# Attention whose probabilities and outputs stay unscaled, with one table of sums that scales the outputs in the gate stage

## The reference, cut to what matters

```
p = jnp.exp(s - m)                                   # s: scores of one head, m: their row maximum
p = p / jnp.sum(p, axis=-1, keepdims=True)           # (guarded against zero)
o_a = einsum('bhqk,bkhd->bqhd', p, v)                # first kind: MLA, 8 heads

o = jnp.stack([o_c, o_s, o_w], axis=-2)              # first kind: NSA, 8 heads, three branches
o = jnp.einsum('bshnd,bshn->bshd', o, sigmoid(gate)) # each branch of each head has its own gate
x = x + (g_a * o_a + g_b * o_b + g_c * o_c) @ w_out  # merge; g_*: sigmoid of a wide product of h
```

## Time and profile before

| what | value |
|---|---|
| median of 3 runs | 3661.39 us (3660.16 to 3663.33) |
| the profiled execution, its span | 3659.4 us |
| what lies around the span, by the median | 2.0 us |
| PE busy | 3522.1 us, 96% |
| DVE busy | 2062.9 us, 56% |
| POOL busy | 1681.8 us, 46% |
| ACT busy | 1399.7 us, 38% |
| mean granted TensorE clock | 0.981 |

### The profile page before, as it was taken

How to read it: one execution, slowest core, us unless ns; L and a number is a source line. 1 busy time by engine, 2 the same in 40 slices (tenths; PEclk the granted TensorE clock), 3 DMA queues, 4 the chain that set the end, 5 groups by cost and what they waited for, 6 DMA issues and landing times. The chain is left out here.

```text
span 3659.4 us, 46833 instructions
## 1 busy us (share of the span) xinstructions
PE 3522.1 (96%) x16596; PEld 2873.6 (79%) x16596; DVE 2062.9 (56%) x3132; ACT 1399.7 (38%) x2450; POOL 1681.8 (46%) x949
## 2 busy tenths in 40 slices
PE   7999999999999999999999999989999999999998
PEld 6876878788878778777888778778877777778877
DVE  5777745212267777461123676558863666648953
ACT  3243652323233446433232436333333446333332
POOL 3347544344434375443444564425443655435543
PEclk9999999999999999999999999989999999999999
DMA  4310023222332110232243220533343220532322
GB/s 162 104 53 29 30 81 115 81 97 92 98 117 93 49 33 24 91 114 89 92 149 126 77 76 24 184 111 120 120 138 122 76 81 28 177 124 104 126 92 92
DMA packets 96756, 346.75 MB, mean 95 GB/s; under 512 B 12624, under 2 KB 13264, under 8 KB 95952
## 3 DMA queue, kind: packets, MB, share of 16 engines
q1 hardware_dynamic: 96592, 344.61, 27.8%
HBM read 338.14 MB, written 6.29 MB: 94 GB/s over the span
## 5 line engine op out<-in xcount | busy, mean ns | idle before, releaser
L226 POOL TENSOR_TENSOR weights_lo<-arena,weights_hi 128x1024 fp32r<-128x1024 f32 x467 | 1175.3, 2517 | 1529.9 <-ACT weights_hi L200 1528.9
L200 ACT ACTIVATE weights_hi<-arena 128x1024 fp32r<-128x1024 f32 x491 | 517.3, 1054 | 627.8 <-PE ps L634 389.8
L294 PE MATMUL ps<-moving_hi,weights_hi 128*128 128x512 f32 x2256 | 568.6, 394 | 11.7 <-ACT weights_hi L200 6.7
L294 PE MATMUL ps<-moving_lo,weights_hi 128*128 128x512 f32 x2256 | 558.5, 390 | 0.0
L294 PE MATMUL ps<-moving_hi,weights_lo 128*128 128x512 f32 x2256 | 558.0, 389 | 0.0
L294 PEld LDWEIGHTS ps<-moving_hi,weights_hi 128*128 128x128 f32 x2256 | 424.9, 189 | 103.5 <-ACT weights_hi L200 7.1
L294 PEld LDWEIGHTS ps<-moving_lo,weights_hi 128*128 128x128 f32 x2256 | 423.8, 188 | 87.6
L294 PEld LDWEIGHTS ps<-moving_hi,weights_lo 128*128 128x128 f32 x2256 | 423.2, 188 | 87.3
L1083 POOL TENSOR_SCALAR arena<-arena 128x128 f32<-128x128 f32 (+2 forms) x240 | 225.0, 950 | 211.0 <-DVE arena L988 131.8
L247 DVE TENSOR_TENSOR moving_lo<-arena,moving_hi 128x512 fp32r<-128x512 f32 x196 | 177.2, 955 | 233.5 <-ACT moving_hi L242 233.5
L2182 DVE SCALAR_TENSOR_TENSOR arena<-ps,arena 128x512 f32 x64 | 44.0, 691 | 306.7 <-PE ps L294 292.5
(11 more groups left out here) (366 smaller groups left out, 5587.2 us busy)
## 6 DMA issues: line engine op xcount, KB each, us to landing
arena<-wstream SPq DMA_DIRECT2D x532, 512.0 KB, 3.4
arena<-modw SPq DMA_DIRECT2D x64, 512.0 KB, 3.8
arena<-modw_first SPq DMA_DIRECT2D x32, 512.0 KB, 4.1
layer_input<-arena SPq DMA_DIRECT2D x2, 2048.0 KB, 6.9
arena<-layer_input SPq DMA_DIRECT2D x2, 2048.0 KB, 8.1
arena<-xT SPq DMA_DIRECT2D x4, 512.0 KB, 5.4
outT<-arena SPq DMA_DIRECT2D x8, 256.0 KB, 2.1
arena<-con SPq DMA_DIRECT2D x1, 1411.5 KB, 9.4
```

Of the source, the lines that this page charges most:

```text
L200: m.nc.scalar.activation(m.w_hi[:, j % 2, :], slab(m, base + at), ACT.Copy).then_inc(hi_ready, 1)
L226: m.nc.gpsimd.tensor_tensor(m.w_lo[:, j % 2, :], slab(m, base + (j if at is None else at)), m.w_hi[:, j % 2, :].bitcast(F32), ALU.subtract)\
L294: mm = m.nc.tensor.matmul(bank, unit_tile(w, k), a[:, k, :], start=(p == 0 and k == 0), stop=(p == 2 and k == KD - 1))
```

## The change

No probability is scaled any more. `invert`, the diagonal and POOL's scaling are gone; all ten blocks are turned by plain transposes (line 921 of the new kernel). The row sums of all units of a layer go into one table, `totals`. In NSA each branch of a head now has an output of its own (`o_branch`), so `product` and `finish` run for every unit by themselves, and ACT's `side` copy too. The gate stage has a new helper, `Shares`: DVE inverts the table, weighs it with the gates, and packs high and low part (`pack`); PE turns it (four transposes of 128 x 64); ACT copies the turned rows and makes a selection matrix (`pick`); then for each output tile of 128 channels (12 in the conv form, 8 in the other, 40 in all) PE spreads the two rows over the partitions with one matmul (`spread`) and DVE multiplies the tile by them (`norm`). POOL adds the two NSA branches. The gate stage rotates over 5 PSUM banks instead of 6, and has 26 semaphores instead of 17.

```diff
@@ attention_stage
             def turn(u):
-                pe.wait_ge(scaled, u + 1)
-                pe.wait_ge(diag_done, u + 1)
+                pe.wait_ge(exped, 3 * u + 3)
...
-                            if qt < TT - 1:
-                                mm = nc.tensor.transpose(o, block, m.ident)
-                            else:
-                                mm = nc.tensor.matmul(o, block, diagonal(u), start=True, stop=True)
+                            mm = nc.tensor.transpose(m.ps[:, bank, c + (qt - kt) * P:c + (qt - kt + 1) * P], prob[:, u % 2, at:at + P], m.ident)
...
             def product(u):
-                if b == 0 and j:
-                    pe.wait_ge(o_out, j)
+                if u:
+                    pe.wait_ge(o_out, u)
...
-            def invert(u):
...
-                nc.vector.reciprocal(rinv[:, s:s + 4], sums[:, s:s + 4]).then_inc(inverted, 1)
...
-                nc.vector.tensor_scalar(diagonal(u), m.ident, rinv[:, s + 3:s + 4], None, ALU.mult).then_inc(diag_done, 1)
...
             def finish(u):        # ACT
-                for j, v in heads_out(u):
-                    act.wait_ge(pv_done, v + 1)
-                    nc.scalar.activation(side[rows(j), :], m.ps[other(j), 6, :], ACT.Copy).then_inc(side_out, 1)
+                j = u // nb
+                act.wait_ge(pv_done, u + 1)
+                nc.scalar.activation(side[rows(j), :], m.ps[other(j), 6, :], ACT.Copy).then_inc(side_out, 1)
...
-                for qt in range(TT - 1):
-                    v = prob[:, u % 2, PROB_AT[qt]:PROB_AT[qt] + P * (qt + 1)]
-                    r = nc.gpsimd.tensor_scalar(v, v, rinv[:, s + qt:s + qt + 1], None, ALU.mult)
-                r.then_inc(scaled, 1)
@@ new: Shares
+    def pack(self, dve, gates=None):
+        nc.vector.memset(self.table, 0.0).then_inc(self.cleared, 1)
+        part = self.totals[:, 0:TT * U]
+        nc.vector.reciprocal(part, part).then_inc(self.weighed, 1)
...
+            for b in range(2):
+                nc.vector.tensor_tensor(shares[:, b], shares[:, b], gates(b), ALU.mult).then_inc(self.weighed, 1)
...
+        nc.vector.tensor_copy(table[:, :, 0:U], by_unit).then_inc(self.packed, 1)
+        dve.wait_ge(self.packed, 1)
+        nc.vector.tensor_tensor(table[:, :, 32:32 + U], by_unit, table[:, :, 0:U].bitcast(F32), ALU.subtract).then_inc(self.packed, 1)
...
+    def spread(self, pe, n):
...
+                pe.wait_ge(self.normed, n)
+            self.m.nc.tensor.matmul(self.bank, self.picks[:, n * P:(n + 1) * P], self.rows, start=True, stop=True).then_inc(self.spread_done, 1)
+    def norm(self, dve, n):
+            dve.wait_ge(self.spread_done, n + 1)
+            self.m.nc.vector.tensor_tensor(self.targets[n], self.targets[n], self.bank, ALU.mult).then_inc(self.normed, 1)
@@ gate_stage
-    count, BANKS = len(rest), 6
+    count, BANKS = len(rest), 5
+    SPREAD = 3 if conv else 1
...
+            shares.pack(dve, lambda b: gn[:, :, :, :, 1 + b])     # ahead of the three adds
...
+            for n in range(len(targets)):                          # ahead of the norm's reciprocal root
+                shares.norm(dve, n)
             dve.wait_ge(rooted, 2)
...
-            weights_lo_loop(pool, m, base, hi_ready, lo_ready, 1, count)
+            for c in range(count):
+                weights_lo(pool, m, base, 0, c, count, hi_ready, lo_ready)
+                if conv and c >= count - 4:
...
+                        nc.gpsimd.tensor_tensor(o, o, targets[2 * pair + b], ALU.add).then_inc(merged, 1)
...
+                for p in range(3):
+                    mm = split_pass(pe, m, base, 0, c, count, m.ps[:, c % BANKS, :], hi_ready, lo_ready, p)
...
+                    shares.spread(pe, 3 * (c - SPREAD) + p)
                 if conv and c == 0:
                     pe.wait_ge(totalled, 3)
                     nc.tensor.matmul(m.ps[:, 6, :], m.ones, sq[:, 0, :], start=True, stop=True).then_inc(summed, 1)
+                if c == 0:
+                    shares.turn(pe)
...
+                if c == 0:
+                    shares.pick(act)
```

More of the change, by code:

```diff
@@ L867, in stacked_keys, with attention_stage @@
         in_turn(pool, cut, m.nc.gpsimd.tensor_tensor(m.r(low)[n:n + 64, :], rows, m.r(high)[half:half + 64, :].bitcast(F32), ALU.subtract))
-def attention_stage(m, nb, terms, values, biases, weights, out, spread, add=False, gates=(), base=0, taps=None, heads=NH):
+def attention_stage(m, nb, terms, values, biases, out, totals, column, gates=(), base=0, taps=None, heads=NH):
     nc = m.nc
@@ L877, in attention_stage @@
     prob, pt, low, side = m.prob, m.pt_hi, m.pt_lo, m.o_side
[L878 to L881, removed]
+    mx = m.small[:, 0:8]
+    with stage(m, "scores maxed exped transposed hi_out lo_out pv_done side_out o_out tapped " + Beside.NAMES) as (block, (
+            scores, maxed, exped, transposed, hi_out, lo_out, pv_done, side_out, o_out, tapped, *side_sems)):
         fill = Beside(m, base, gates, 7, side_sems)
@@ L1002, in finish @@
             def finish(u):
-                for j, v in heads_out(u):
[L1004 to L1014, removed]
+                j, b = divmod(u, nb)
+                dve.wait_ge(side_out, u + 1)
+                nc.vector.tensor_tensor(out(b, j // 2)[rows(j), :], m.ps[rows(j), 6, :], side[rows(j), :], ALU.add).then_inc(o_out, 1)
             rowmax(0)
-            invert(0)
             for u in range(NU):
@@ L1069, in _ @@
             chunks_out(NU)
-            finish(NU)
+            finish(NU - 1)
             fill.ahead(act)
@@ L2000, in gate_stage @@
+def gate_stage(m, base, rest, logits, totals, units, targets, modulate=False, conv=False):
     nc = m.nc
-    count, BANKS = len(rest), 6
+    count, BANKS = len(rest), 5
+    SPREAD = 3 if conv else 1
     x = lambda c: m.conv[:, c, :]
@@ L2019, in _ @@
         def _(dve):
-            for n in later:
-                rest_modulation(m, dve, n, 0, mod_added)
             if not conv:
+                shares.pack(dve)
+                for n in later:
+                    rest_modulation(m, dve, n, 0, mod_added)
+                    for k in range(3 * n, 3 * n + 3):
+                        shares.norm(dve, k)
                 return
+            gn = m.gn.rearrange("p (t a r n) -> p t a r n", t=TT, a=4, r=2)
+            shares.pack(dve, lambda b: gn[:, :, :, :, 1 + b])
             total = sq[:, 0, :], sq[:, 1, :]
@@ L2047, in _ @@
         def _(pool):
-            weights_lo_loop(pool, m, base, hi_ready, lo_ready, 1, count)
+            for c in range(count):
+                weights_lo(pool, m, base, 0, c, count, hi_ready, lo_ready)
+                if conv and c >= count - 4:
+                    pair = c - (count - 4)
+                    o = m.o_nsa[:, pair, :]
+                    for b in range(2):
+                        pool.wait_ge(shares.normed, 2 * pair + b + 1)
+                        if b:
+                            pool.wait_ge(merged, 2 * pair + 1)
+                        nc.gpsimd.tensor_tensor(o, o, targets[2 * pair + b], ALU.add).then_inc(merged, 1)
             if count % 2 == 0:
```

122 lines of the change are left out of this document (72 added, 50 removed).

## The result

Median of five runs 3691.21 us (3685.85 to 3709.00), against 3663.06 before: ratio 1.0083, interval 1.0064 to 1.0103. The change makes the kernel 28 us slower; forecast were 13, and 3691 lies above the range. The profiled execution is the slowest of the five: span 3706.8 at a mean clock of 0.971, where the four others have 0.976 to 0.977 and the profiled execution before has 0.981.

What follows compares the result with a forecast made beforehand. TensorE, busy 96% of the span, was taken as the bound. Terms -24.0 + 10.0 + 2.0 + 2.5 + 11.4 + 9.0 + 2.0 = +12.9 us gave 3674 us, range 3654 to 3686.

Steps and rivals of the forecast that it cites:

- Attention: All attention stages: transposes replacing fp32 products save TensorE 35.2 us, of which 24.0 us remain net.
- the loop: MLA attention: VectorE and ScalarE steps, 6.49 us a unit, set the pace; 5.9 us of the saving lost.
- The stalls in units without a pass: 16-unit attention stages: TensorE waits for the loop before units without a gate pass, 1.2 us more per NSA stage.
- Rival (b): Faster, 3643 us: the loop shortens without reciprocals and attention's saving comes out in full; chance 0.07.
- (d): Attention's clock falls with all-transpose turns: a half-clock stretch in each of six stages, 10 us, 3684; chance 0.05.
- The spreads: Gate stages: 40 matmuls of 128 x 512 at 0.25 us each add 10.0 us (8 to 20).
- the other gates: Non-conv gate stages, twice: norms and modulation sums share VectorE and the merge clock may fall, 2.0 us together.
- rival (c): Much slower, 3688 us: both conv stalls at their long end, each with two half-clock stretches; chance 0.08.
- The start of the conv stage: Conv gate stages: packing blocked by GpSimd's low parts stalls TensorE 4.0 us, plus 1.7 of clock; 11.4 us for two.
- Rival (a): Even, 3657 us: blocking does not pile up, conv stages start 0.5 us late, no half-clock stretch; chance 0.24.
- The end of the conv stage: Conv gate stages: layer norm behind twelve norms delays the end 2.8 us, plus 1.7 of clock; 9.0 us for two.
- The clears: Start of four merges: nine more GpSimd clears make TensorE wait 0.63 us longer each, 2.5 us in all.

Runs made afterwards that it cites:

- the pair of runs with 64 and 96 rows: Kernel before plus 40 unused matmuls of 64 or of 96 rows at the spreads' places, five gate banks: 3690.29 us and 3676.69 us.
- the first edit alone: Layer norm's reciprocal (in halves) and next steps put between the last four conv norms, on the changed kernel with spreads of 96 rows: 3669.81 us, ratio 1.0014.
- both together: GpSimd's adds of branches two chunks earlier, on the kernel with all four edits (layer norm between the norms included): 3651.00 us, ratio 0.9973.
- all four edits: Changed kernel with spreads of 96 rows, totals ahead of the pack, layer norm between the last norms, 16 gate semaphores: 3654.99 us, ratio 0.9975.

## Why the prediction was wrong

**Attention: right.** 35.2 us of work went, 25.0 came out, 24.0 were forecast. Two side copies of MLA after (for rows 5):

```profile
269.60 0.59 ACT L1007 ACTIVATE arena<-ps 64x512 f32<-64x512 f32 x1
...
275.99 0.59 ACT L1007 ACTIVATE arena<-ps 64x512 f32<-64x512 f32 x1
```

They are 6.39 us apart, the loop's length and no longer TensorE's, as the runs without taps show. The stalls in units without a pass came too:

```profile
431.79 1.64 PE L931 MATMUL ps<-split,split 128*128 128x512 f32 x8 [0.87 <-ACT split L1029]
```

Rival (b) falls with this. So does (d), which has one stretch at half clock in each of the six stages: with all ten blocks of a turn transposed there are three such stretches of 3.4 us in the six stages, where before there were two. The clock there is 0.97 to 1.00 after and 0.98 to 1.00 before. The Trainium skill's rule on transposes (TensorE: Matmul & The Clock Gate, "Part 4: PE-mode transpose") does not show here.

**The spreads: the step that failed.** The prediction said "With a semaphore wait ahead I take 0.25: 10.0 us (8 to 20, the latter at 0.50 ...)". They cost 0.66 each, 26 in all: 16 us over the value and 6 over the upper end. With 26 in place of 10 the same sum gives 3690. The rest about cancels: the stalls and the other gates came out smaller than taken, the clock larger. I priced the spread by its columns and looked to waits for a surcharge; what it costs is the change of height. (Even the 0.20 was low: that stretch of the earlier trace rows counts matmuls that its ends cut. A pass of eight takes 1.81 us, 0.23 each.) The kernel before shows this price, in a stage that the prediction did not read, where products of 37 rows stand between passes of 128:

```profile
233.35 2.11 PE L403 MATMUL ps<-moving_lo,weights_hi 128*128 128x512 f32 x8
235.40 0.47 PE L1370 MATMUL ps<-split 37*96 37x512 f32 x1
235.71 0.39 PE L1371 MATMUL ps<-split,split 37*96 37x512 f32 x1
...
236.63 0.39 PE L1371 MATMUL ps<-split,split 37*96 37x512 f32 x1
236.95 2.11 PE L403 MATMUL ps<-moving_hi,weights_lo 128*128 128x512 f32 x8
```

Between themselves they are 0.23 apart. The first takes 0.31, the last 0.32, and the pass of eight 2.05 and not 1.81: 0.4 us for one way there and back. For a single spread that more than doubles its price. The Trainium skill (TensorEngine Tiling (Array Packing), "Tiling Modes") says that changing the tiling mode, which splits the array's 128 rows in two halves of 64 or four of 32, drains TensorE. I had not weighed it. Both traces and the pair of runs with 64 and 96 rows agree with it: a matmul of 96 rows goes like one of 128, one of 64 does not. That a plain matmul of 64 rows changes the mode is my reading of these rows; no run shows the mode itself. The kernel before even shows that 66 rows are enough, in the second kind of attention:

```profile
2245.63 0.39 PE L930 MATMUL ps<-arena 128*128 128x128 f32 x2
2245.85 1.02 PE L913 MATMUL ps<-arena 66*128 66x512 f32 x2
2246.71 0.22 PE L914 MATMUL ps<-arena 128*128 128x128 bf16 x1
```

The steps of 0.22 and 0.86 are those of MLA, where the same two products have 96 rows (1280.75, 1280.97, 1281.83).

The time came close to rival (c)'s 3688 for another reason than (c)'s, and that is luck: neither conv stall was at its long end.

**The start of the conv stage: right in mechanism, too large.** The stall was 2.56 us, ended by VectorE, behind GpSimd's low parts; I took 4.0. The third add did not meet another low part. One of the two was followed by a stretch at half clock, not both. Rival (a), with a stall of 0.5 us and no such stretch, falls with this. The port rule of the prediction (the Trainium skill, SBUF — State Buffer, "SBUF: two separate sides") agrees: the multiplies of two SBUF inputs lasted as long as GpSimd's instructions, the norms with an input from PSUM took 0.69 as forecast, also when they lay wholly within one (487.89, within L226 from 487.27 to 489.67).

**The end of the conv stage: right.** The stage ended 2.7 us behind TensorE's last matmul, 0.1 before; 2.8 was taken. Two causes add up, the late reciprocal and GpSimd's adds: the first edit alone left 1.0 us, both together 0.1. Earlier adds alone were not run.

**The clears: right in waits, wrong in clock.** Nine clears added 0.93 us to the wait of two merges and 0.64 to that of the other two (I took 0.63). But I gave the clock 0.5 us in each of the other merges, and there it took about 3.3. The longer wait does not do that by itself: at the start of these merges the clock fell only in the kernels with spreads of 64 rows. All four merges together lost 14.5 us, against 6.9 in the forecast.

**The clock as a whole.** At 0.981 of 3659 us TensorE had 139 us at half clock before; at 0.977 of 3687, the four runs without the accident, 170: 31 more, 15 us lost at most, since TensorE stood idle in part of them. Forecast were 7.8. So of the 28 us about half are work and stalls and up to 15 clock. This split is rough: later executions of the kernel before have clocks of 0.978 to 0.981, and one in the middle of them, 0.980, makes the 15 a 12.

## What to carry to other kernels

Price a small matmul put between large ones by its neighbours, not by its columns: look in the trace for any place where the heights change and measure both edges there. If it is of 64 rows or fewer and alone, fill it with zero rows; here that gave back 15 of 28 us. Write the zeros where no engine is waited for: here they cost 1.2 us in each of two stages. Where a change makes one engine faster, find the loop of the other engines that lies just below before counting the gain, and count each added semaphore as a clear in the next stage's start.

## What the hardware showed that was not expected

- Matmuls of 37 and 64 rows beside ones of 128 pay at both edges (0.31 to 0.32 us before, 0.32 to 0.43 behind, in place of 0.23). Those of 31, 32 and 24 rows come 0.32 behind a matmul of a pass too, one of 80 rows only 0.23. Those of 96 rows don't pay (0.23 on either side), nor do those of 66, by the rows above, so the line lies between 64 and 66 rows.
- The weight load shows it as well: that of a spread of 64 rows starts with its matmul (both at 515.44), that of one of 96 rows 0.23 ahead of it (488.81 and 489.04).
- At a merge's start the length of the wait alone did not settle the clock. Behind waits of 1.47 to 1.76 us the first matmuls ran at full clock in every merge; behind 2.47 in the changed kernel, and behind 2.70 in the kernel with all four edits, at half; behind 2.48 with 96 rows, and behind 3.42 with the layer norm between, at full, in the latter for 1.3 us.
- A stage that no edit touches lost 12 us once, at a clock of 0.68. One execution is not enough to read a few us of clock from.
